# Layer 0's recurrence between weight pieces on two PSUM banks, and layer 1's suffix sums in fp32 with the mask on VectorE

## The reference

```python
o_inter = einsum('bhck,bhkv->bhcv', qd, S)
S = exp(bl)[..., None] * S + einsum('bhck,bhcv->bhkv', kt, vv)
```

```python
z = einsum('bqhd,bkhd->bhqk', q, k) * scale + bias
log_fail = where(mask, log_sigmoid(-z), 0.0)
after = cumsum(log_fail, reverse=True) - log_fail
w = where(mask, exp(log_sigmoid(z) + after), 0.0)      # then w @ v
```

## Time and profile before

| | us |
|---|---|
| runs (three) | 1792.76, 1794.27, 1803.53; median 1794.27 |
| profiled execution, its own time | 1795.47 |
| its span, first to last instruction | 1793.7 |
| TensorE busy | 1607.4 (90%) |
| VectorE busy | 753.8 (42%) |
| ScalarE busy | 630.6 (35%) |
| GpSimd busy | 568.7 (32%) |
| mean granted TensorE clock | 0.918 of 2.4 GHz |

### The profile page before, as it was taken

The page is one execution under the profiler, slowest core; times in us unless marked ns, Lnnn a source line. Parts: engine busy times, 40 slices in busy tenths (PEclk is TensorE's granted clock), DMA queues, the critical chain, the costliest instruction groups (busy, mean ns, idle before and its releaser), DMA issues.

```text
span 1793.7 us, 25351 instructions
## 1 busy us (share of the span) xinstructions
PE 1607.4 (90%) x9409; PEld 1243.0 (69%) x9409; DVE 753.8 (42%) x1039; ACT 630.6 (35%) x1069; POOL 568.7 (32%) x472
## 2 busy tenths in 40 slices
PE   6679998786797998999989979999888999999997
PEld 4457665563475775767766546656568999999996
DVE  2561002324376767667767793014332321221221
ACT  3421223412224441444234342245533442342341
POOL 1221221100042433333333344322213444444443
PEclk9887899857798999999999989987799999999999
DMA  8472896843254889998996988621002233332322
GB/s 250 156 243 84 278 351 221 287 144 118 94 190 129 259 280 307 307 312 279 320 348 215 330 271 270 205 88 47 1 24 71 71 95 95 88 89 85 95 83 88
DMA packets 288755, 325.96 MB, mean 182 GB/s; under 512 B 13814, under 2 KB 205952, under 8 KB 288436
## 3 DMA queue, kind: packets, MB, share of 16 engines
q1 hardware_dynamic: 145800, 215.89, 36.3%
q10 hardware_dynamic: 140512, 100.67, 18.5%
q0 software_dynamic: 2320, 7.78, 1.2%
HBM read 315.48 MB, written 8.99 MB: 181 GB/s over the span
## 4 chain that ended last, share of the span: by engine, by line
PE 72%; DVE 11%; DMA 5%; ACT 5%; issue 3%; SPq 3%; POOL 1%; ACTq 0%; DVEq 0%; POOLq 0%
PE PS L513 46%; PE PS L527 5%; PE PS L552 3%; PE PS L472 2%; DMA wring<-w_ffn_up 2%; PE PS L822 2%; PE PS L462 2%; SPq L1210 2%; PE PS L1036 1%; DVE prod L2240 1%; DVE scr L1966 1%; DVE hl_r L1973 1%; PE PS L570 1%; PE PS L584 1%; DVE scr L2245 1%
## 5 line engine op out<-in xcount | busy, mean ns | idle before, releaser
L1334 POOL TENSOR_TENSOR parts<-wring,parts 128x512 fp32r<-128x512 f32 (+1 forms) x400 | 520.4, 1303 | 1106.6 <-ACT parts L1412 1106.0
L513 PE MATMUL PS<-hh_r,parts 128*128 128x260 f32 (+1 forms) x2880 | 716.7, 338 | 20.6 <-DVE hl_r L1973 11.6
L513 PEld LDWEIGHTS PS<-hh_r,parts 128*128 128x128 f32 x2880 | 494.7, 191 | 109.9 <-issue 53.4
L1412 ACT ACTIVATE parts<-wring 128x512 fp32r<-128x512 f32 (+1 forms) x400 | 248.0, 623 | 809.8 <-PE PS L513 681.0
L513 PE MATMUL PS<-hl_r,parts 128*128 128x260 f32 (+1 forms) x1440 | 462.5, 334 | 0.0
L513 PEld LDWEIGHTS PS<-hl_r,parts 128*128 128x128 f32 x1440 | 275.5, 191 | 27.6 <-issue 1.7
L513 PE MATMUL PS<-E_r,parts 128*128 128x260 f32 (+1 forms) x1584 | 261.8, 325 | 4.4 <-issue 2.4
L513 PEld LDWEIGHTS PS<-E_r,parts 128*128 128x128 f32 x1584 | 227.6, 191 | 43.6 <-issue 20.9
L2240 DVE TENSOR_TENSOR prod<-kring,PS 128x1024 f32<-128x1024 f32 x128 | 150.1, 1214 | 28.3 <-DMA kring<-cache_sb_k 28.0
L2245 DVE TENSOR_REDUCE scr<-prod 128x16 f32<-128x1024 f32 x128 | 149.7, 1211 | 0.0
L2422 DVE TENSOR_TENSOR xT<-xT,PS 128x512 f32<-128x512 f32 (+1 forms) x64 | 44.1, 690 | 199.1 <-PE PS L513 199.1
(11 more groups left out here) (313 smaller groups left out, 1560.3 us busy)
## 6 DMA issues: line engine op xcount, KB each, us to landing
vring<-cache_sb_v SPq DMA_DIRECT2D x256, 256.0 KB, 4.1
kring<-cache_sb_k SPq DMA_DIRECT2D x256, 256.0 KB, 4.2
wring<-w_ffn_up ACTq DMA_DIRECT2D x88, 512.0 KB, 5.3
wring<-w_ffn_down ACTq DMA_DIRECT2D x16, 1024.0 KB, 5.7
kring<-w_ffn_up SPq DMA_DIRECT2D x12, 1024.0 KB, 9.8
vring<-w_ffn_up SPq DMA_DIRECT2D x10, 1024.0 KB, 10.1
wring<-w_in_gla ACTq DMA_DIRECT2D x8, 1024.0 KB, 8.3
wring<-w_out ACTq DMA_DIRECT2D x8, 1024.0 KB, 5.0
```

Of the source, the lines that this page charges most:

```text
L513: last = mm(PS[:, bank + c, 0:w], parts[:, q, a, P * k:P * k + P], x[:, k0 + kk, o:o + w], start=(q == 0 and k == 0 and a == 0 and x is sr ...
L1334: gp.tensor_tensor(part_as(n, 1, src, w), src, part_as(n, 0, src, w), ALU.subtract).then_inc(wlo_ok, 1)
L1412: return fn(dst, src, ACT.Copy)
```

## The change

Layer 0. The value panels move ahead of the memory-query and gate panels, so that the order is query and key rows, low-rank gate, values, memory queries, gate rows. Pieces 16 to 23 use only banks 0 and 1; the recurrence uses banks 2 and 3 and is cut into seven parts (`gla_step`), one behind each of the pieces 16 to 22. The chunk updates run in two halves, because two banks hold four chunks. Attention, states, outputs and transposed keys move to `scr`; the chunk-end decays are copied to a small tile `ebl`; the softmax tiles of layer 0's memory attention move to `E`. GpSimd masks one head behind the weight parts of each of the pieces 17 to 20. The Silu over the gate rows follows the loop over pieces. Steps 4 to 79 move to earlier positions: positions 2 to 23 take what 24 to 31 had.

Layer 1. The suffix sums are taken in fp32 from one unrounded tile with fp32 triangle and ones; rounded copy, remainder and constant copies go. The softplus tile has four buffers where it had two. The negative triangle is no longer added by TensorE: VectorE adds it to the diagonal blocks after moving the scores out.

The diff, cut to its core (renamed loops, repeated bodies and the accounting of banks are left out):

```diff
-GIN = ((0, 256, 1024, 1280, 1552, 1808), (0, 256, 512, 768, 1536, 1792))
+GIN = ((0, 256, 1552, 1808, 1024, 1280), (0, 256, 512, 768, 1536, 1792))
+VP = (6, V0)
-S_AT = [2, 2] + [2] * 6 + [3] * 12 + [3] * 4 + [2] * 8 + [4, 3, 2, 2, 1]
+S_AT = [2, 2] + [3] * 6 + [4] * 9 + [5] + [3] * 5 + [2] + [0] * 8 + [4, 3, 2, 2, 1]
...
+        ebl = sb("ebl", [P, 2, NCH])
-        raw_o = hlF[:, 0:4, 0:SEQ]
-        att = hhf[:, 4 * TOK:4 * TOK + 2048].rearrange("p (h t n) -> p h t n", h=4, t=4)
+        raw_o = scr[:, 0:2048].rearrange("p (h n) -> p h n", h=4)
+        att = scr[:, 0:2048].rearrange("p (h t n) -> p h t n", h=4, t=4)
...
-        sbt = [ringF[:, SBW * p:SBW * p + SBW] for p in range(2)]
-        sb_hi, sb_lo = ([ringR[:, SBW * (a + p):SBW * (a + p) + SBW] for p in range(2)] for a in (2, 4))
-        identR, onesR, triR, laterR = (ringR[:, 6 * SBW + P * k:6 * SBW + P * k + P] for k in range(4))
+        sbt = [ringF[:, SBW * p:SBW * p + SBW] for p in range(4)]
...
+            def gla_step(n):
...
+                if n == 0:
+                    pe.wait_ge(qk_ok, 1)
+                    for b in (2, 3):
+                        pe.wait_ge(dense_free[b], pl.dense[b])
+                    attention(0)
+                    attention(1)
+                elif n == 1:
+                    attention(2)
+                    attention(3)
+                elif n == 2:
+                    pe.wait_ge(ke_ok, 1)
+                    for j, B in ((0, B4), (1, B6)):
+                        tr_unit(B, ("keT", j), [(P * t, ke[:, j, P * t:P * t + P]) for t in range(TT)])
+                elif n == 3:
+                    pe.wait_ge(att_out, 4)
+                    B4.read(pe, ("keT", 0))
+                    B6.read(pe, ("keT", 1))
+                    for c in range(4):
+                        last = updates(c)
+                    last.then_inc(kv_done, 1)
+                elif n == 4:
+                    pe.wait_ge(kv_read, 1)
+                    for c in range(4, 8):
+                        last = updates(c)
+                    last.then_inc(kv_done, 1)
+                elif n == 5:
+                    pe.wait_ge(st_ok, 1)
+                    outputs(0)
+                    outputs(1)
+                elif n == 6:
+                    outputs(2)
+                    outputs(3)
+
+            def in_projection_gla():
+                for i in range(4):
+                    fm_piece(0, IN0 + i // 2, i % 2, i, (hh, hl), 0, PROMPT, h_split(0) if i == 0 else None)
...
+                for p in range(2):
+                    token_panel(0, VP[0] + p, range(4), (hh, hl), 4 * p, p == 0, p == 1, between)
+                for i in range(4, 12):
+                    fm_piece(0, IN0 + 2 + i // 2, i % 2, i, (hh, hl), 0, PROMPT, None, i % 2)
+                    gla_step(i - 4)
+                    if 5 <= i < 9:
+                        norm_sums(("mq", 0, i - 5), [B6], 1, cuts(PROMPT))
+                    after_piece()
+                for h in range(4):
+                    norm_sums(("gla", h), [B6], 1, cuts(PROMPT))
...
                     for kc in range(TT):
                         w = SEQ - P * kc
-                        mm(PSf[:, SBO[kc]:SBO[kc] + w], zT[r:r + 64, 4 + j, P * kc:P * kc + P],
-                           zT[r:r + 64, j, P * kc:SEQ], start=True, stop=False)
-                        last = mm(PSf[:, SBO[kc]:SBO[kc] + P], identR, laterR, start=False, stop=True)
+                        last = mm(PSf[:, SBO[kc]:SBO[kc] + w], zT[r:r + 64, 4 + j, P * kc:P * kc + P],
+                                  zT[r:r + 64, j, P * kc:SEQ], start=True, stop=True)
...
-                    pe.wait_ge(splo_ok, h + 1)
+                    x = sbt[h % 4]
+                    pe.wait_ge(spr_ok, h + 1)
...
-                        for x in parts_:
-                            last = mm(PSf[:, o:o + w], triR, x[:, SBO[kc]:SBO[kc] + w], start=(x is parts_[0]),
-                                      stop=(kc == TT - 1 and x is parts_[1]))
+                        last = mm(PSf[:, o:o + w], tri[:, :], x[:, SBO[kc]:SBO[kc] + w], start=True, stop=(kc == TT - 1))
                         for k2 in range(kc + 1, TT):
                             w2 = SEQ - P * k2
-                            for x in parts_:
-                                last = mm(PSf[:, o + P * (k2 - kc):o + P * (k2 - kc) + w2], onesR,
-                                          x[:, SBO[k2]:SBO[k2] + w2], start=False, stop=(k2 == TT - 1 and x is parts_[1]))
+                            last = mm(PSf[:, o + P * (k2 - kc):o + P * (k2 - kc) + w2], ones[:, :],
+                                      x[:, SBO[k2]:SBO[k2] + w2], start=False, stop=(k2 == TT - 1))
...
-                pe.wait_ge(sbc_ok, 1)
                 scores(0)
...
+                    if l == 0 and h % 2 and 17 <= 2 * j + h // 2 < 21:
+                        gla_mask(2 * j + h // 2 - 17)
...
+                    if i in (16, 17):
+                        for h in (2 * (i - 16), 2 * (i - 16) + 1):
+                            act.wait_ge(att_done, h + 1)
+                            copy(att[:, h], PS[:, 2 + h % 2, :].rearrange("p (t n) -> p t n", t=TT)).then_inc(att_out, 1)
...
+                    if i == 11:
+                        act.wait_ge(s_st, 64)
+                        B4.get(act, "gd")
+                        copy(gdT, PS[0:GR, 4, :]).then_inc(B4.free, 1)
...
-                def high(h):
-                    act.wait_ge(spr_ok, h + 1)
-                    if h >= 2:
-                        act.wait_ge(r_done, h - 1)
-                    copy(sb_hi[h % 2], sbt[h % 2]).then_inc(sphi_ok, 1)
...
                     ts(sbz[h % 4], PSf[:, 0:SBW], SBD ** -0.5, sbb[:, h:h + 1], ALU.mult, ALU.add).then_inc(z_read, 1)
+                    dve.wait_ge(z_read, h + 1)
+                    for o, n in ((0, 512), (896, 128)):
+                        blocks = sbz[h % 4][:, o:o + 2 * n].rearrange("p (a n) -> p a n", a=2)[:, :, 0:P]
+                        last = tt(blocks, blocks, later[:, :].rearrange("p (a n) -> p a n", a=1).to_broadcast((P, 2, P)), ALU.add)
+                    last.then_inc(sbc_ok, 1)
```

More of the change, by code:

```diff
@@ new lines, in in_projection_gla @@
+            def in_projection_gla():
+                for i in range(4):
+                    fm_piece(0, IN0 + i // 2, i % 2, i, (hh, hl), 0, PROMPT, h_split(0) if i == 0 else None)
+                    if i == 2:
+                        mem_keys(0, (B4, B6))
+                    if i == 3:
+                        pe.wait_ge(wg_ok, 1)
+                        B4.put(pe, "gd")
+                        for k in range(KD):
+                            for a, hs in ((0, (hh, hl)), (1, (hh,))):
+                                for x in hs:
+                                    last = mm(PS[0:GR, 4, :], wgp[:, a, k, :], x[:, k, 0:SEQ], start=(k == 0 and a == 0 and x is hh),
+                                              stop=(k == KD - 1 and a == 1))
+                        last.then_inc(B4.full, 1)
+                    after_piece()
@@ L1672, in mix_in @@
-                    if i == 4:
-                        act.wait_ge(kss_ok, l + 1)
-                        tables(LNEXP)
-                        steps.link(fn(s_kn, s_kn, ACT.Ln, scale=1.0 / P, bias=eps[:, 0:1]))
-                        fn(s_kn, s_kn, ACT.Exp, scale=-0.5).then_inc(kr_ok, 1)
-                    if i == 7:
-                        if l:
-                            act.wait_ge(tail_st, 112)
-                        piece_out(base + i)
-                        for t in range(MT):
-                            copy(memV[:, t, :], PS[:, 2 + t, :]).then_inc(dense_free[2 + t], 1)
@@ L1715, in gla @@
+                for b in range(2):
+                    act.wait_ge(dense_free[b], dense_uses(0, "in", 10 + b))
                 fn(zT[:, 4:8, 0:SEQ], zT[:, 4:8, 0:SEQ], ACT.Silu).then_inc(eg_ok, 1)
                 tables("silu")
[L1717 to L1722 removed]
                 tables(LNEXP)
@@ L1829, in sb_constants @@
                 act.wait_ge(v_used, 64)
-                for dst, src in ((identR, ident), (laterR, later), (triR, tri), (onesR, ones)):
-                    last = copy(dst, src[:, :])
-                last.then_inc(sbc_ok, 1)
             def mem_exp(h):
@@ new lines, in states @@
+            def states(first):
+                dve.wait_ge(kv_done, 1 if first == 0 else 2)
+                for n in range(first, first + 4):
+                    c = 256 * (n // 2 % 2)
+                    kv = PS[:, 2 + n % 2, c:c + 256].rearrange("p (j v) -> p j v", j=2)
+                    if n == 0:
+                        link(copy(S[:, 0], kv))
+                        continue
+                    for j in range(2):
+                        last = stt(S[:, n, j, :], S[:, n - 1, j, :], ebl[:, j, n:n + 1], kv[:, j, :], ALU.mult, ALU.add)
+                    if n == 3:
+                        last.then_inc(kv_read, 1)
+                        dve.wait_ge(kv_read, 1)
+                    elif n < NCH - 1:
```

(22 more changed lines are left out.)

443 lines of the change are left out of this document (216 added, 227 removed).

## The result

| | before | after |
|---|---|---|
| median of 20 runs each | 1796.36 us | 1780.43 us |
| ratio, 95% interval | | 0.991 (0.989 to 0.9929) |
| profiled execution, span | 1793.7 us | 1782.5 us |
| TensorE busy, mean granted clock | 1607.4 us, 0.918 | 1593.0 us, 0.930 |

A ratio compares the fast executions only: one that takes over 1.5% more than the fastest of its kernel is left out.

What follows compares the result with a forecast made beforehand. TensorE is busy nearly everywhere, so only its idle time and low clock could be cut. Layer 0 -15.7, layer 1's head -9.9 and loop -7.7 sum to -33.3, from 1795.5 to 1762 us; range 1738 to 1795.

Steps and rivals of the forecast that it cites:

- Head: Layer 1 attention before the first suffix sum: 17.7 us with TensorE itself as the limit, a gain of 9.9 us.
- the first head's other path: Layer 1's head: PSUM move, mask, ScalarE passes and VectorE, done by about 1208, before the first sum at 1211.5; not binding.
- Loop: Layer 1's loop over eight heads: 57.3 us of work at clock 0.87 plus 8 us waits, 73.9 us, gaining 7.7.
- Sums: Layer 1's fp32 suffix sums: half the columns at a higher price, 4.45 us per head at full clock.
- The estimate of 5.84 us by four passes: Layer 1's sums per head at four to one, 11 us more over eight heads, forecast 1775; set aside for 4.45.
- The reason that I gave for the clock: Layer 1's loop: score products using 64 of 128 rows shrink from 18.6 to 11 us, so clock 0.87 for 0.75.
- the gross gain of 28.7 us: Layer 0: steps and recurrence leave the 74.6 us stretch; their matmuls between pieces at clock 0.85 take 45.9 us.
- Rival B: Layer 0 gives nothing: recurrence keeps half clock and waits, full DMA engines hold four-step positions; 1778, up to 1783; chance 0.19.
- the term for transfers: Layer 0: at four positions, four steps' panels and half a weight panel outlast TensorE's work; cost 3 us (0 to 6).
- Answers: Layer 0: recurrence parts behind pieces wait for ScalarE or VectorE at some five more places; cost 7 us (0 to 14).
- Silu: Layer 0's gate Silu after the last piece: some 2 us of ScalarE, covered by two steps, otherwise costing those 2 us.
- Cover of the sample chain: Layer 0: dependent steps 16 to 21 move behind two half panels, with 5.6 us less cover; cost 3 us (0 to 6).

Runs made afterwards that it cites:

- either edit of the old scores: Two runs on the kernel before: layer 1's score products contracted over 128 rows (0.9941), or each head's identity products placed after its score products (0.9932).
- grouped_new: Changed kernel with each head's layer 0 outputs reordered, the four 128-row products first, then the seven 64-row state products, nothing padded; 0.9843 of before.
- grouped_best: Kernel before with layer 1's change, layer 0's outputs grouped by shape in the old recurrence, and layer 1's queries padded to 128 rows; 0.9721 of before.
- old_l1_grouped: Kernel before with layer 1's four score products of a head first and its four identity products after them; 0.9932 of before.
- padded_old: Kernel before with layer 1's change and layer 0's queries zero-padded so the old recurrence's state products contract over 128 rows; 0.9733 of before.

## Why the prediction was right and wrong

**Layer 1: right in its sums, in part by luck.** Head: 17.7 us, as summed, but not by the path that I gave. I had TensorE as the limit throughout, at half clock and with 0.9 us of waiting, and the first head's other path off it. In the chain that path binds: the transposes, and with them the next scores, wait for mask, ScalarE's passes and its copy until 1213.0. TensorE is idle for 3.7 of the 17.7 us, and its clock is 0.77. Two errors cancel here. Loop: 57.3 / 0.87 + 8 = 73.9 was forecast; found were 73.85, as 66.45 x 0.89 = 59.1 us of work and 7.4 idle. The work and the waits are right; that the clock is met to 0.02 is luck, as eight of ten profiles of this code have 0.93 or 0.94. Sums: 4.45 us per head forecast, 4.53 found (1256.06 to 1260.59 in the chain). The estimate of 5.84 us by four passes came out too high because I multiplied the wrong row: 0.57 ns per column is the price of the old sums' short rounded products, while the weight pieces' take 5.69 us / (24 x 512) = 0.46 ns. Of that, 1.74 ns is 3.8 times as much. The Trainium skill, page "FP8 and Floating Point Precision", section "TensorE Precision Notes", gives true FP32 four passes through the array. By the pieces' rows, at 3.8, the trace agrees. The mask is not wholly hidden: in the head it stands in the chain with 0.77 us. The reason that I gave for the clock is only partly right: either edit of the old scores gives the old loop 3.6 to 4.1 of its 7.75 us, by one profile each. I take the rest to come from ScalarE's rounding copies, which went: its busy time fell from 44.9 to 36.7 us, and TensorE's waits for its exponential are 7.4 us instead of 11.5. No run takes the copies away alone, so this is not shown.

**Layer 0: the failed step is the gross gain of 28.7 us**, namely "the recurrence's output matmuls are small and follow one another without a piece inside a group, so I take 0.85". I read half clock as the price of missing pieces and moved the matmuls, with their cause, to where pieces are. In the new order the cause is the alternation of 128-row and 64-row products inside the outputs, and it came along: 0.73 from 341.7 to 397.0 instead of 0.85, and pieces 22 and 23 now pay for it too (7.0 and 6.6 us for 5.69). Padding gave 16.9 us back in that stretch and 18.3 in the stage; grouping by shape also kept the clock up. Rival B had the outcome ("the recurrence drags half clock and its waits along, and full DMA engines hold the four-step positions") at a chance of 0.19, and both its halves are shown. The second step that failed is the term for transfers.

**The other terms.** Transfers: 3 (0 to 6) forecast; halving them gave 9.8 back in 212.7 to 341.7, and 9.5 over the stage with the clock mended. I had set four panels against one position, while several four-step positions follow each other at 331 GB/s and a wait also costs clock. Answers: 7 on top of the old 5.5 forecast, 7.9 in all found. Silu: 0 to 2 forecast; from the last products ahead of the output norms to the last norm TensorE idles for 5.4 us, where it was 2.4 (before: 401.1 to 410.8, 9.70 us with 7.34 busy), so 3. Cover of the sample chain: 3 forecast, 4.7 left at piece 21. Together, as an estimate from these runs: a recurrence among pieces at 0.96 would take 39.0 / 0.96 = 40.6 for 74.6, -34.0; clock +16.9, transfers +9.8, answers +2.4, Silu +3.1 and cover +4.7 leave +2.9, where +1.4 was measured. The gross gain is thus 17.1 us instead of 28.7, and the new waits are 20 instead of 13. The terms of 2 to 5 us come from single profiles, and the stage alone scatters by 1.8 us with the new order and 8.9 with the old, so the near agreement of the sum proves none of them.

**The range** held the time, but its likeliest part (1750 to 1777) did not: layer 1's part, forecast at 17.6 us, was all that the change gave.

## What to carry to other kernels

Before moving work out of a stretch at half clock, find which instructions are in it and ask whether they take the low clock along. In these kernels products on 64 rows between products on 128 rows were dear twice, by their own time and by the clock behind them. Padding the contraction with zeros mended both wherever it was tried in layer 0; grouping products of one shape did so only where the clock was high on entry. A prefetch that is just covered on average is not covered where the busiest positions follow each other. And before a term is called right, or an edit's gain real, look at the same stage in every profile that has the same code there.

## What the runs showed of the hardware

- At full granted clock one 128-row product and two 64-row ones in turn took 1.00 us, with 128 rows in all three 0.67; a head's four and seven, grouped by shape, took 2.6 us.
- TensorE fell from 2.4 to 1.2 GHz while it was busy without a gap, with alternating products behind a piece that had ended at full clock: 1.00 from 348.85 to 354.2 and 0.59 from there to 357.3. The Trainium skill, page "TensorE: Matmul & The Clock Gate", section "What's actually happening", says that the gate is set by how busy the engine has been lately. If the profile's busy share is taken for that, the trace does not agree: 53.6 of 55.3 us busy gave 0.73, and 36.7 of 38.4 gave 0.96.
- In the profiled executions grouped products on 64 rows kept a high clock (`grouped_new`) and did not raise a low one (`grouped_best`, 0.50 from 345 to 378, and the head of `old_l1_grouped` at 0.51). Layer 0's products padded to 128 rows did (`padded_old`, full clock within the first head).
